# Strassen's scheme for 24 of the 32 slabs of the up projection of a decoder step

## What is computed

```python
D_MODEL = 1024
...
D_FF = 4 * D_MODEL
...
    f = jnp.square(jax.nn.relu(x @ w1 + b1)) @ w2 + b2
    x = layer_norm(DN_ALPHA * x + f, ln3_g, ln3_b)
```

## Time and profile before

| | us |
|---|---|
| median of 3 runs | 1383.34 (1382.68 to 1383.98) |
| profiled execution | 1379.41 |
| its span, first to last instruction | 1377.6 |
| PE busy in the span | 1326.0 |
| up stage from its third slab to the first down unit | 661.44 to 1010.04 |

### The profile page before, as it was taken

How to read it: one execution, slowest core, us unless ns; L and a number is a source line. 1 busy time by engine, 2 the same in 40 slices (tenths; PEclk the granted TensorE clock), 3 DMA queues, 4 the chain that set the end, 5 groups by cost and what they waited for, 6 DMA issues and landing times.

```text
span 1377.6 us, 21845 instructions
## 1 busy us (share of the span) xinstructions
PE 1326.0 (96%) x8744; PEld 1279.3 (93%) x8744; DVE 882.5 (64%) x1034; ACT 431.9 (31%) x821; POOL 783.7 (57%) x576
## 2 busy tenths in 40 slices
PE   6999999999999999999999999999999999989995
PEld 6999988788899978889999999999999999989995
DVE  5899994456612762387664246324469998897767
ACT  4223442245612441145211131112243444422233
POOL 3476987544933714629433337333359999994522
PEclk9999999989999999999999999999999999999998
DMA  8222452110020266201233433333343133346112
GB/s 257 69 51 45 126 162 78 31 46 1 32 61 31 76 234 239 80 16 46 79 93 93 156 93 93 93 93 140 140 162 109 58 110 125 110 158 206 57 47 81
DMA packets 59018, 136.91 MB, mean 99 GB/s; under 512 B 21568, under 2 KB 27968, under 8 KB 56512
## 3 DMA queue, kind: packets, MB, share of 16 engines
q1 hardware_dynamic: 49184, 132.99, 29.7%
q10 hardware_dynamic: 9760, 2.93, 0.9%
HBM read 107.02 MB, written 28.88 MB: 99 GB/s over the span
## 4 chain that ended last, share of the span: by engine, by line
PE 62%; DVE 27%; issue 3%; POOL 3%; DMA 2%; ACT 2%; SPq 0%; DVEq 0%; ACTq 0%; POOLq 0%
PE bank L809 20%; PE bank L810 19%; PE bank L811 19%; DVE bank L1901 11%; DVE ffn_sum L2404 2%; POOL w_low L759 2%; DVE form_low L2372 1%; DVE weight_sums L2388 1%; DVE product_sums L2404 1%; DMA form_full<-hidden 1%; DVE bank L2028 1%; DVE x_full L2018 1%; DVE x_full L2035 1%; DVE form_full L2366 1%; ACT x_full L1613 1%
## 5 line engine op out<-in xcount | busy, mean ns | idle before, releaser
L809 PE MATMUL bank<-x_high,w_high 128*128 128x384 f32 (+1 forms) x1200 | 391.0, 326 | 14.5 <-POOL w_low L475 11.3
L810 PE MATMUL bank<-x_low,w_high 128*128 128x384 f32 (+1 forms) x1200 | 388.3, 324 | 0.0
L811 PE MATMUL bank<-x_high,w_low 128*128 128x384 f32 (+1 forms) x1200 | 387.6, 323 | 0.0
L809 PEld LDWEIGHTS bank<-x_high,w_high 128*128 128x128 f32 x1200 | 226.0, 188 | 17.0 <-POOL w_low L475 10.1
L473 POOL TENSOR_TENSOR w_high<-w_raw,ones 128x1024 fp32r<-128x1024 f32 x48 | 92.0, 1916 | 240.4 <-issue 128.9
L811 PEld LDWEIGHTS bank<-x_high,w_low 128*128 128x128 f32 x1200 | 226.1, 188 | 0.0
L810 PEld LDWEIGHTS bank<-x_low,w_high 128*128 128x128 f32 x1200 | 226.1, 188 | 0.0
L2435 DVE TENSOR_TENSOR relu<-relu 128x384 f32<-128x384 f32 (+1 forms) x96 | 96.6, 1010 | 187.6 <-ACT relu L1807 187.6
L809 PE MATMUL bank<-form_high,w_high 128*128 128x264 f32 x672 | 192.5, 286 | 5.1 <-DVE product_sums L2404 2.0
L810 PE MATMUL bank<-form_low,w_high 128*128 128x264 f32 x672 | 191.5, 285 | 0.0
L811 PE MATMUL bank<-form_high,w_low 128*128 128x264 f32 x672 | 190.5, 283 | 0.0
(11 more groups left out here) (285 smaller groups left out, 2698.9 us busy)
## 6 DMA issues: line engine op xcount, KB each, us to landing
w_raw<-slabs_in SPq DMA_DIRECT2D x110, 512.0 KB, 3.7
dec_kv<-dec_kv_in SPq DMA_DIRECT2D x16, 1024.0 KB, 6.0
hidden<-relu SPq DMA_DIRECT2D x24, 528.0 KB, 5.3
form_full<-hidden SPq DMA_DIRECT2D x24, 528.0 KB, 6.6
mix<-hidden SPq DMA_DIRECT2D x16, 528.0 KB, 5.7
hidden<-relu_low SPq DMA_DIRECT2D x8, 528.0 KB, 3.9
hidden<-unit_high SPq DMA_DIRECT2D x8, 528.0 KB, 4.9
scratch<-slabs_in SPq DMA_DIRECT2D x8, 512.0 KB, 3.9
```

The source lines that it names most:

```text
L809: pe.matmul(out, w_high, x_high, start=first, stop=False)
L810: pe.matmul(out, w_high, x_low, start=False, stop=False)
L811: return pe.matmul(out, w_low, x_high, start=False, stop=last)
```

## The change

Of the 32 slabs of the up stage, 24 become 12 units of two output blocks, four k-blocks by two, and two halves of the tokens (528 each). Each unit has seven products (`up_product`) in place of eight; a product is two halves of 264 columns by four k-blocks by three matmuls, 24 in all, into one of four pairs of banks. `UP_ORDER` gives the forms in the order of the products. In the text, a unit's products are counted first to seventh in that order. The eight other slabs run as before, four ahead of the units ("W1") and four behind ("W1B"); they are the hidden blocks that are kept as high and low.

- The forms of x: four sums of whole quarters (2112 elements a partition, `xs_full`), made once by DVE during the first four slabs, cast by ACT (`x_high`), split by DVE (`x_low`).
- The weights of a unit fill both raw slots. DVE makes four sums of 512 columns (`up_weight_sums`), ACT casts seven forms (`up_high`, four slots, each free when the product four before is done), POOL makes seven low parts (`up_low`). SP loads the next unit's two halves when POOL has read the sixth and the seventh form.
- The products: ACT copies the first to SBUF (`up_copy`), DVE makes seven sums of products (`up_sum` in `up_unit`), four of them in place in PSUM, ACT applies relu (`up_relu`) and now also squares, in the slabs too. The next unit's four weight sums stand on DVE between the third and the fourth product sum.
- ACT begins the residual blocks (`sum_begin`), DVE completes them (`sum_set`): five within units 3 to 7, three after.
- The first group's forms for the down stage are loaded after the units; POOL's `form_low(0, ...)` stand after the seventh and the eighth slab's split.

```diff
-LATE = LAST - NU
+VU = (UP - NB) // 2
+V_ST = S_FF + NB
+S_UP, S_FB = S_FF + 4, S_FF + 4 + 2 * VU
+LATE = LAST - NU - 2 * VU
+UP_ORDER = (0, 5, 1, 2, 6, 3, 4)
+UP_READ, UP_SUM = {0: 1, 1: 2, 3: 3, 4: 4, 6: 5}, {2: 2, 5: 4}
+X_FORM = {2: 0, 1: 1, 3: 2, 4: 3}
...
-STAGES += [("W1", times(16, SIX), (2, 5)), ("ST", {}, ()), ("W2", *LINEAR), ("C3", LN_MEAN, ()), ("T3", SIX, ())]
+STAGES += [("W1", times(2, SIX), (2, 5)), ("UP", {}, ()), ("W1B", times(2, SIX), (2, 5)), ("ST", {}, ()), ("W2", *LINEAR), ("C3", LN_MEAN, ()), ("T3", SIX, ())]
...
+    def up_source(V, i):
+
+        o = {0: raw[:, 0, 0:512], 3: raw[:, 0, 512:1024], 5: raw[:, 1, 0:512], 4: raw[:, 1, 512:1024]}
+        return o[i] if i in o else up_sums[:, {2: 0, 1: 1, 6: 2}[i], :]
...
-            if j == 9:
+        for V in range(VU):
+            for p in range(2):
+                sp.wait_ge(sem("w_form_low"), 7 * V + 6 + p)
+                sp.wait_ge(sem("weight_sums"), 4 * (V + 1))
+                load(S_UP + 2 * V + 2 + p, p)
+            pair_out(V)
+        for j in range(4, NB):
+            sp.wait_ge(split_done, S_FF + j + 1)
+            load(S_FB + j - 2, j % 2)
+            if j == 4:
                 forms_in(0)
+            hidden_out(j)
         for U in range(NU):
...
+        def up_low(f):
+
+            pool.wait_ge(sem("w_form_high"), f + 1)
+            pool.tensor_tensor(wl_up[:, f % 4, :], up_source(f // 7, UP_ORDER[f % 7]), wh_up[:, f % 4, :].bitcast(f32), ALU.subtract)\
+                .then_inc(sem("w_form_low"), 1)
+
...
+        for j in range(4, NB):
+            if j < 6:
+                pool.wait_ge(sem("st_done"), 7 * VU - 2 + 2 * (j - 4))
+            split(S_FF + j, j % 2, (S_FB + j - 4) // 2, MEM_SLABS, freed=S_FF + 4 if j < 6 else S_FF + j - 1)
+            if j == 6:
+                form_low(0, 0)
+                form_low(0, 4)
+            if j == 7:
+                form_low(0, 5)
+                form_low(0, 6)
...
-        pairs("W1", S_FF, 1, UP // 2, x_parts)
+        pairs("W1", S_FF, 1, 2, x_parts)
+
+        def up_product(f):
+
+            V, q = divmod(f, 7)
+            i, k = UP_ORDER[q], f % 4
+            pe.wait_ge(sem("w_form_low"), f + 1)
+            if V == 0 and i in X_FORM:
+                pe.wait_ge(sem("form_low_dve"), i)
+            if f < 4:
+                for n in (2 * k, 2 * k + 1):
+                    take(n, FREED["UP"][n])
+            else:
+                v, r = divmod(f - 4, 7)
+                if r in UP_READ:
+                    pe.wait_ge(sem("up_read"), 5 * v + UP_READ[r])
+                else:
+                    pe.wait_ge(sem("up_sums"), 7 * v + UP_SUM[r])
+            high, low = (xs_high[:, X_FORM[i]], xs_low[:, X_FORM[i]]) if i in X_FORM else (x_quarter(xh, i), x_quarter(xl, i))
+            for c in range(2):
+                t = slice(c * HT // 2, (c + 1) * HT // 2)
+                for kb in range(4):
+                    w = slice(kb * P, (kb + 1) * P)
+                    last = product(ps[2 * k + c][:, 0:HT // 2], wh_up[:, k, w], wl_up[:, k, w], high[:, kb, t], low[:, kb, t],
+                                   kb == 0, kb == 3)
+            last.then_inc(sem("st_done"), 1)
+
+        for f in range(7 * VU):
+            up_product(f)
+        pe.wait_ge(sem("up_read"), 5 * VU - 1)
+        pairs("W1B", S_FF + 4, 0, 2, x_parts)
...
+        def up_high(f):
+
+            V, q = divmod(f, 7)
+            i = UP_ORDER[q]
+            if f < 4:
+                act.wait_ge(used, S_FF + 3 + f // 2)
+            else:
+                act.wait_ge(sem("st_done"), f - 3)
+            if i in (0, 5, 4):
+                act.wait_ge(*up_raw(V, 0 if i == 0 else 1))
+            else:
+                act.wait_ge(sem("weight_sums"), 4 * V + {2: 1, 3: 2, 1: 3, 6: 4}[i])
+            act.copy(wh_up[:, f % 4, :], up_source(V, i)).then_inc(sem("w_form_high"), 1)
...
+        def up_relu(V, q, n, p, a):
+
+            act.wait_ge(sem("up_sums"), 7 * V + n)
+            if q in (1, 3):
+                act.wait_ge(sem(f"hidden_out{p}"), pairs_out(V - 1))
+            y = relu[:, p, a:a + HT]
+            act.activation(by_banks(y), pair(7 * V + q), ACT.Relu, bias=col("b1", 2 * V + p)).then_inc(sem("up_read"), 1)
+            act.wait_ge(sem("up_read"), 5 * V + UP_READ[q])
+            act.activation(y, y, ACT.Square).then_inc(sem("square"), 1)
...
+        for j in range(4):
+            up_block(j)
+            if j == 1:
+                x_high(0)
+                x_high(1)
+            if j == 2:
+                up_high(0)
+                up_high(1)
+                x_high(2)
+        up_high(2)
+        up_high(3)
+        x_high(3)
+        for f in range(7 * VU):
+            V, r = divmod(f, 7)
+            if f + 4 < 7 * VU:
+                up_high(f + 4)
+            if r == 0:
+                up_copy(V)
+            elif r == 1:
+                up_relu(V, 1, 1, 0, 0)
+            elif r == 5:
+                up_relu(V, 3, 5, 1, HT)
+                up_relu(V, 4, 6, 0, HT)
+            elif r == 6:
+                up_relu(V, 6, 7, 1, 0)
+            elif r == 3 and 2 <= V < 7:
+                if V == 2:
+                    act.wait_ge(sem("hidden_out1"), pairs_out(0))
+                sum_begin(V - 2)
+        for j in range(4, NB):
+            if j == NB - 1:
                 for i in range(4):
...
+            up_block(j)
+            if j == 4:
+                act.wait_ge(sem("w_form_low"), 7 * VU)
+                act.wait_ge(sem("up_sums"), 7 * VU)
+                sum_begin(5, 6, 7)
...
+        def up_weight_sums(V):
+
+            b11, b12, b21, b22 = raw[:, 0, 0:512], raw[:, 0, 512:1024], raw[:, 1, 0:512], raw[:, 1, 512:1024]
+            t1, t2, t4 = (up_sums[:, k, :] for k in range(3))
+            for p in range(2):
+                dve.wait_ge(*up_raw(V, p))
+            if V:
+                dve.wait_ge(sem("w_form_low"), 7 * V - 2)
+            else:
+                dve.wait_ge(used, S_FF + 2)
+            for k, (out, x, y, op) in enumerate(((t1, b12, b11, ALU.subtract), (b12, b22, b12, ALU.subtract), (t2, b12, b11, ALU.add),
+                                                 (t4, b21, t2, ALU.subtract))):
+                if k:
+                    dve.wait_ge(sem("weight_sums"), 4 * V + k)
+                tt(out, x, y, op).then_inc(sem("weight_sums"), 1)
...
+        def up_unit(V):
+
+            d, e, g = (by_banks(up_part[:, k, :]) for k in range(3))
+            m2, m6, m5, m4, m7, m3 = (pair(7 * V + q) for q in range(1, 7))
+            dve.wait_ge(sem("up_read"), 5 * V + 1)
+            up_sum(V, 1, m2, m2, d, 2)
+            up_sum(V, 2, e, m6, d, 3)
+            if V == 0:
+                x_low(3, 4)
+            up_sum(V, 3, g, m5, e, 4, 2)
+            if V + 1 < VU:
+                up_weight_sums(V + 1)
+            up_sum(V, 4, e, m7, e, 6, 3)
+            up_sum(V, 5, m5, m5, e, 0, 4)
+            up_sum(V, 6, m4, m4, e, 0, 4)
+            up_sum(V, 7, m3, m3, g, 7)
+            if 2 <= V < 7:
+                sum_set(V - 2)
...
+        dve.wait_ge(used, S_FF)
+        dve.wait_ge(sem("x_norm_low"), 6 * NB)
+        s1, s2, s3_, s4 = (xs_full[:, k] for k in range(4))
+        own.link(tt(s4, h21, l21, ALU.add))
+        own.link(tt(s1, s4, h22, ALU.add))
+        tt(s1, s1, l22, ALU.add).then_inc(sem("form_sums"), 1)
+        block_low(0)
+        own.link(tt(s3_, h11, l11, ALU.add))
+        dve.wait_ge(sem("form_sums"), 1)
+        tt(s2, s1, s3_, ALU.subtract).then_inc(sem("form_sums"), 1)
+        block_low(1)
+        tt(s3_, s3_, s4, ALU.subtract).then_inc(sem("form_sums"), 1)
+        dve.wait_ge(sem("form_sums"), 3)
+        own.link(tt(s4, l12, s2, ALU.subtract))
+        x_low(1, 2)
+        x_low(0, 2)
+        up_weight_sums(0)
+        block_low(2)
+        tt(s4, s4, h12, ALU.add).then_inc(sem("form_sums"), 1)
+        x_low(2, 3)
+        block_low(3)
+        for V in range(VU):
+            up_unit(V)
+        dve.wait_ge(sem("w_form_low"), 7 * VU)
+        for j in range(4, NB):
+            if j == NB - 1:
+                unit_weight_sums(1, 0, 1, 2, 3)
+            if j == 4:
                 form_sums(0, 2, 3, 1, 4)
-            if j == UP - 2:
-                dve.wait_ge(sem("acc_set"), NB)
+            if j == 5:
+                form_low(0, BY_DVE_FORMS[0])
+            block_low(j)
+            for b in ((5,), (6, 7), (), ())[j - 4]:
+                sum_set(b)
+            if j == 6:
+                form_low(0, BY_DVE_FORMS[1])
+                form_low(0, BY_DVE_FORMS[2])
                 unit_weight_sums(0, 0, 1, 2, 3)
-            if j in (16, 17, 18):
-                form_low(0, BY_DVE_FORMS[j - 16])
...
+    up = blocks(w1[0])
+    halves = up[:UP - NB].reshape(VU, 2, P, 2, SLAB // 2).transpose(0, 3, 2, 1, 4).reshape(2 * VU, P, SLAB)
+    ff = [up[UP - NB:UP - NB + 4], halves, up[UP - NB + 4:], quarters, blocks(down[GROUPS * 4 * P:])]
```

176 lines of the change are left out of this document (102 added, 74 removed).

## The result

| | before | after |
|---|---|---|
| median of 4 runs, us | 1383.01 (1382.53 to 1383.98) | 1373.50 (1370.64 to 1374.33) |
| ratio | | 0.9927 (95% interval 0.9909 to 0.9944) |
| profiled execution, its span | 1379.41, 1377.6 | 1374.33, 1372.5 |

A forecast was written before the change was run, and what follows sets the result against it. PE, busy 96% of the span, was taken as the bound. -32.9 + 12.9 + 1.7 + 7.2 + 1.0 + 3.0 = -7.1 us, from 1383.34 to 1376.2 us; band 1369 to 1384 (chance 0.52), range 1361 to 1391.

The forecast's parts named there:

- PE: 24 slabs against 12 bare units: Up stage: 278.9 us of slabs replaced by 245.9 us of unit products, a gain of 32.9 us if none waits.
- first unit late: First unit: DVE's sums for forms of x and the work behind them delay PE, 12.9 us, 8 to 18 allowed.
- clock after the rest: After the first unit: PE's clock falls following its long rest, costing 1.7 us once.
- ten crossings: Unit starts from the second unit on: PE waits 0.72 us at each of ten, 7.2 us in all.
- fifth slab's start: End of the units: sums, relus and a square after the sixth product free the first bank late, 1.0 us.
- last slab and down stage's head: Last four slabs and first down unit: form loads and low parts come late, 3.0 us, 0 to 6.
- the chain: Each unit: second raw slot's load, four weight sums, fourth and fifth product sums, relu; 21.22 us against PE's 20.50.
- the meeting: Each unit: DVE's second weight sum stands still during one POOL operation, charged 1.29 us.
- The first rival: Crossings: weight sums precede POOL's lock or loads land in 3.3 us, so crossings are free; -18.6, 1364.7 us; chance 0.22.
- The second rival: Units: second raw slot's load bounds them; break-even landing 4.55 us; at 5.3 us, 9.0 us slower, 1392.3 us; chance 0.18.
- POOL and DVE in turns: First unit: the two engines alternate, so the last form of x is ready only at 697.8.
- Half a us at the first down unit: Head of the down stage: half a us of waiting, counted within the 3.0 us for the tail.

The follow-up runs named there:

- the second execution: The changed kernel itself, unmodified, measured again as yardstick: 1371.46 us, ratio to before 0.9936.
- e1: Changed kernel with the next unit's four weight sums behind the sixth product sum, and ACT's dependent cast behind the relus: 1361.86 us, ratio to before 0.9871.
- e7: Changed kernel with one added wait: POOL's low part of a unit's second weight form waits for the four weight sums: 1364.53 us, ratio to before 0.9882.
- e2: Changed kernel with the weight sums moved behind the sixth product sum in the first unit only: 1365.48 us, ratio to before 0.9890.
- e8: Changed kernel with two of DVE's eight sums for the forms of x left out: 1364.91 us, ratio to before 0.9878.
- e5: Changed kernel with residual blocks 6 and 7 set by DVE behind the second down unit's weight sums: 1369.53 us, ratio to before 0.9913.
- e12: e10 with the third unit's weight sums behind the seventh product's sum in the first down unit: 1356.89 us, ratio to before 0.9813.
- e6: Changed kernel with DVE's and ACT's work reordered ahead of and in the first unit, no work added or removed: 1371.62 us, ratio to before 0.9924.
- e10: e9 with a third order of work at the head, including the orders of e6: 1358.29 us, ratio to before 0.9825.
- e9: e1 with the high parts of three slabs cast by ACT instead of made by POOL: 1356.39 us, ratio to before 0.9807.

## Why the prediction was right, and where its terms were off

| term of the sum | forecast, us | measured in the trace after, us |
|---|---|---|
| PE: 24 slabs against 12 bare units | -32.9 | 278.9 - 244.9: -34.0 |
| first unit late | +12.9 | +9.3 |
| clock after the rest | +1.7 | about +2.4 of the second unit's 2.7 |
| ten crossings | +7.2 | +4.8 and what is left of the 2.7 (the 4.8 is 3.1 in the second execution) |
| fifth slab's start | +1.0 | +1.2 |
| last slab and down stage's head | +3.0 | 1.6 + 3.6 = +5.2 |

The sum of the right column is about -10.7, beside -9.5 between the medians. It does not close on the traces it is taken from: their spans differ by 5.1 us, since the execution after came to its first unit 2.9 us late and lost 2.8 more behind the product at 1014.18. Neither is a term of the forecast.

**PE's gain** was right to 1.1 us: a product takes 2.92, not 2.93.

**The crossings.** The mechanism was the forecast's: units 0.2 to 1.2 us longer than bare, their next matmul released by ACT's relu, with one long weight sum. e1 took the chain away and the waits went to 0.00; e7 took the meeting away and they went to 0.09 at most. The size was off by the term of the meeting, 1.29 charged and 0.97 to 1.13 measured, and by the load, which usually landed 3.5 us after POOL's end and not 3.84; where it landed later, units of 21.6 stand, above the forecast's 21.22. The first rival (the chain hides) lay nearer than its 0.22 said: at 0.34 us a crossing in the second execution, half the forecast was hidden. The second rival's mechanism is there, since the landing does pass on to the period one for one, but the landing of 4.55 us that it needed was not reached in any of the nine.

**The first unit.** Its order of events was as worked out, and DVE began where the sum said. The third product came 1.8 us late (2.4 forecast), but the fifth 2.7 (6.4), and the seventh low part 3.1 us earlier than forecast. The term that was too large is DVE's way to the last form of x, which ended 33.0 us after the third slab's start (664.34) and not 36.4. DVE's third weight sum and that last sum show where:

```profile
691.43 0.69 DVE L2629 TENSOR_TENSOR up_weight_sums<-w_raw 128x512 f32<-128x512 f32 x1
...
693.93 3.42 DVE L2687 TENSOR_TENSOR x_form_full<-x_form_full,x_high 128x2112 f32<-128x2112 f32 x1
```

Of the 3.4 us, 1.1 were gained by the end of the first form's split (the opening meeting with POOL cost 3.7 us, 4.4 charged), 0.6 up to the third weight sum, and 1.7 behind it, where "POOL and DVE in turns" took 5.2 us and not 6.9. From the seventh low part on, 3.84 + 6.42 were forecast and 3.49 + 6.20 measured. About half of the first unit's wait hangs on this last chain, the same as at the crossings: e2 moved the weight sums in this unit alone, and 4.7 us went. Two sums less on DVE took 4.5 away (e8). The two were not run together, so it is not shown that they add up to the whole.

**The tail.** The last slab was as forecast, 36.4 us after the fifth and so 1.5 late, behind two form low parts. "Half a us at the first down unit" failed: it was 3.6. Two of DVE's residual sums and a cast of ACT in the trace after, and DVE's weight sum before:

```profile
981.59 2.94 DVE L2661 SCALAR_TENSOR_TENSOR ffn_sum<-x_low,ffn_sum 128x1056 f32<-128x1056 f32 x1
990.81 2.86 DVE L2664 TENSOR_TENSOR ffn_sum<-ffn_sum 128x528 f32<-128x528 f32 x1
999.06 0.71 ACT L1890 CAST w_high<-weight_sums 128x256 fp32r<-128x256 f32 x2 [11.03 <-DVE weight_sums L2561]
...
1019.71 1.07 DVE L2388 TENSOR_TENSOR weight_sums<-w_raw 128x256 f32<-128x256 f32 x1 [2.91 <-DMA w_raw<-slabs_in]
```

About half falls in the first down unit. The residual blocks 6 and 7 took DVE 12.1 us beside POOL (981.59 to 993.67; in e5, away from POOL, 4.3). So DVE's weight sums came late, ACT waited 11.03 us for them, and the last slab's relus, which free the banks, stand behind that cast. In e5 the waits for these relus went to 0.00, and a wait for product sums took their place. The other half falls in the second unit and is the crossings' pattern again, weight sums that wait for a load ahead of sums that free banks (1011.64, 3.76 us of idle on DVE), together with a store that left late because DVE was late; e12 moved the sums and this wait went. Before, the same sums waited too (idle 2.91 us at 1019.71), but 9.7 us after the down stage's start and not 13.0. The remaining waits of the down stage, idle of 0.2 to 1.5 us at each change of group, differ between executions of the same code, and nothing here settles why.

**The range.** The time lies in the lower half of the forecast's own band (1369 to 1384). The errors had both signs: 3.6 us too much at the head, about 2 too much at the crossings, 1.1 too little for PE's gain, 2.2 too little at the tail, and nothing for the 5.7 us outside its terms. So the mechanisms were right, and that the number came within 2.7 us of the median is in part luck.

## What to carry to other kernels

Where one engine both prepares the next step and finishes the present one, the finishing operations that free a buffer go first; here a move of four operations past three others was worth as much as the whole algorithm had brought. Two engines that hold one another up count as one in a plan: at the head another order alone only moved the wait (e6), and two sums less shortened it by 4.5 us (e8). Order still counts: with the later weight sums and with work taken from POOL, a third order took 2.2 us from the head (e10 against e9). And an added wait can make a kernel faster if it keeps a long operation from standing in the way of a short one on the chain.

## What was not expected of the hardware

A wait of POOL for DVE's sums was worth 6.9 us between the medians and 5.0 in the traces, since a two-input DVE operation of 0.69 us takes 1.66 to 1.82 when a POOL operation begins beside it. And PE's clock fell after a shorter rest than the 2.4 us that the forecast had reckoned with: behind rests of 6.39, 4.67, 2.41 and 1.91 us the second unit ran partly at 1.2 GHz (23.2, 22.2, 22.0 and 22.2 us), behind 1.50 to 1.68 us it took 20.50 us at 1.00. The length of the rest alone does not decide it. Behind 2.56 us ahead of the first unit's sixth product in e6 the clock stayed at 1.00 (first line); behind 1.92 us ahead of the same product of the second down unit it stayed there in the first execution of the changed kernel (second line) and fell in its second (the two last). What else decides it is not shown.

```profile
703.58:705.50 1.92, 1.92 (x16) 1.92 (x17) 1.92 (x2) 1.04 (x2) 0.80 (x1) 1.00 1.05 383
...
1016.00:1018.00 2.00, 2.00 (x19) 2.00 (x18) 1.17 (x2) 0.00 (x0) 0.00 (x0) 1.00 0.85 340
...
1011.36 0.36 PE L873 MATMUL bank<-form_high,w_high 128*128 128x264 f32 x1 [1.92 <-DVE ffn_sum L2577]
1013.00:1015.00 2.00, 2.00 (x11) 2.00 (x11) 1.43 (x3) 0.00 (x0) 0.00 (x0) 0.50 0.95 379
```
